# Token mixers among the projection tiles of a decoder trunk, and half of the last normalisation on GpSimd

## The reference

```
h = x @ w_in                    # 2816 columns: ret q,k,v,gate | swa q,k,v | conv value,gate | sgu u,v
A  retention, 4 heads x 64: chunks of 128 rows, a = (q k^T) * decay, o = a v + (q S) * q_dec,
   S = S * c_dec + (k * k_dec)^T v ; group norm of o, times silu(gate)
B  attention, 4 heads x 64, causal, log-multiplicity bias; the samples also read cached keys and values
C  val * sigmoid(gate) -> depthwise convolution of width 31 -> layer norm over 256 channels -> silu
D  u, v = gelu ; group norm of v ; u * (W_s v + b) within 128 rows
x = layer_norm(alpha * x + concat(A, B, C, D) @ w_out)
x = layer_norm(alpha * x + moe(x))          # best 1 of 4 groups, then best 2 of its 8 experts
```

## Time and profile before

| | |
|---|---|
| median of 3 runs (lowest to highest) | 1935.23 us (1932.53 to 1937.45) |
| the profiled execution's own time | 1938.98 us |
| its span in the profile | 1936.9 us |
| its mean granted clock of TensorE | 0.854 |
| busy: PE, weight load, DVE, ACT, POOL | 76%, 52%, 28%, 11%, 21% |
| moved by DMA | 532.60 MB, mean 275 GB/s |

### The profile page before, as it was taken

One profiled execution on the slowest core, in us unless ns is written; L12 is line 12 of the kernel. 1 busy time (PEld: TensorE's weight loads), 2 busy tenths in 40 slices (PEclk: granted clock), 3 DMA queues, 4 the chain that ended last, 5 costly groups with the idle time before them and its releaser, 6 DMA issues. The chain is left out here.

```text
span 1936.9 us, 40042 instructions
## 1 busy us (share of the span) xinstructions
PE 1472.9 (76%) x16276; PEld 1012.2 (52%) x16276; DVE 544.6 (28%) x1215; ACT 208.8 (11%) x579; POOL 398.8 (21%) x533
## 2 busy tenths in 40 slices
PE   8998899949567576767499988995766758566990
PEld 7887647835334333434488874684433424333550
DVE  0395352541000000000609735236100101000116
ACT  2111030001000000000121112201000000000010
POOL 3149230111001011100311943001211101110113
PEclk9999589969788888879699977896878878887995
DMA  8711041949999999999531102265899999999824
GB/s 341 280 66 58 1 159 64 364 173 359 428 425 382 425 426 425 384 425 386 194 135 66 44 36 109 92 256 225 333 427 425 380 427 424 426 425 425 349 89 142
DMA packets 77409, 532.60 MB, mean 275 GB/s; under 512 B 14430, under 2 KB 31770, under 8 KB 48538
## 3 DMA queue, kind: packets, MB, share of 16 engines
q1 hardware_dynamic: 45466, 482.00, 60.4%
q0 software_dynamic: 11136, 35.40, 5.0%
q10 hardware_dynamic: 20736, 14.18, 2.3%
HBM read 772.37 MB, written 35.98 MB: 417 GB/s over the span
## 5 line engine op out<-in xcount | busy, mean ns | idle before, releaser
L871 PE MATMUL ps<-arena,xT 128*32 128x256 f32 x6912 | 477.8, 437 | 252.1 <-DMA arena<-in_w 250.5
L871 PEld LDWEIGHTS ps<-arena,xT 128*32 128x32 f32 x6912 | 274.9, 126 | 444.7 <-issue 352.9
L542 PE MATMUL ps<-arena,xT 128*128 128x256 f32 x1920 | 424.9, 382 | 0.9 <-issue 0.9
L542 PEld LDWEIGHTS ps<-arena,xT 128*128 128x128 f32 x1920 | 363.9, 191 | 51.5 <-issue 1.0
L1496 DVE COPY xT<-ps 128x128 f32<-128x128 f32 x108 | 31.5, 291 | 907.2 <-PE ps L880 907.2
L889 PE MATMUL ps<-arena,xT 128*32 128x256 f32 x3456 | 212.2, 386 | 34.0 <-DVE xT L1496 22.4
L1674 POOL COPY xT<-xT 128x1 int32 x108 | 19.7, 182 | 805.8 <-PE ps L861 805.8
L889 PEld LDWEIGHTS ps<-arena,xT 128*32 128x32 f32 x3456 | 108.7, 110 | 110.2 <-issue 27.2
L1676 POOL DMA_INDIRECT xT<-x1d,xT x108 | 105.0, 972 | 53.1 <-POOL xT L1674 49.6
L1106 DVE SCALAR_TENSOR_TENSOR arena<-arena 128x784 f32<-128x784 f32 x120 | 113.7, 1029 | 0.0
L1017 ACT ACTIVATE xT<-ps 128x128 f32<-128x128 f32 x108 | 30.0, 278 | 668.7 <-PE ps L871 668.7
(11 more groups left out here) (244 smaller groups left out, 1223.1 us busy)
## 6 DMA issues: line engine op xcount, KB each, us to landing
arena<-in_w SPq DMA_DIRECT2D x324, 2048.0 KB
arena<-in_w_proj SPq DMA_DIRECT2D x30, 1024.0 KB, 5.0
arena<-in_kv SPq DMA_DIRECT2D x32, 640.0 KB, 5.1
yd<-xT ACTq DMA_DIRECT2D x432, 32.0 KB
yd<-arena POOLq DMA_DIRECT2D x22, 512.0 KB, 18.6
rowpar<-in_rowpar SPq DMA_DIRECT2D x2, 2708.0 KB, 17.2
x1d<-arena SPq DMA_DIRECT2D x8, 512.0 KB, 14.6
arena<-x1d SPq DMA_DIRECT2D x8, 512.0 KB, 6.7
```

The lines of the kernel that those rows point to most:

```text
L542: ins = pe.matmul(bank[0:n, 0:CW], xT[:, k, 128 * t:128 * t + n], ring[slot(c)][:, k, :], start=(k == 0), stop=(k == KT - 1))
L871: ins = pe.matmul(HB[q][r, 0:256], xgT[q][:, k % 2, BLK * (k // 2):BLK * (k // 2 + 1)], w13[q][:, :, k, 128 * j:128 * (j + 1)], start=(k = ...
```

## The change

**Chunks and tiles.** The chunks are taken in another order (VAL, GATE, SQ, SK, SV, RQ, RK, V, RV, U, RG). `chunk` becomes `tile(c, t)`, one row tile of one chunk, on two PSUM banks instead of five (`ps[2]`, `ps[3]`), which leaves `ps[4]` to `ps[7]` to the mixers while projections still run. The ring has one slot that is used once (chunk 2) and two that alternate. PE's list is now: VAL, GATE pairs; SQ, SK, SV with the GLU and attention transposes between; the attention loop with one tile of RQ, RK or V in each unit, the convolution's transposes in units 10 to 14, and the samples' keys, probabilities and values in units 1, 3, 8, 9, 12 and 14; then retention with tiles of RV and U; gating; RG's tiles between the turned rows; the output projection.

**Places.** The transposed heads get buffers of their own in the arena, where x and the fourth cache slot lie (`sT`, `rT`). So x is overwritten and loaded again before the output projection: layer 0 from `x_in`, layer 1 from a DRAM copy `x2d` that SP stores tile by tile in the passage.

**Engines.** The SWA rotation, key decay and retention's norm go from POOL to DVE, the query copies from POOL to ACT; DVE's taps are cut into pieces, 38 before attention and the rest in units 0 to 8. POOL's rotation is six operations for all tiles instead of four for each tile and two. V is copied out and its GELU done at once, behind attention.

**Routing.** 50 products without use (`run_idle`) stand in PE's list in front of three waits.

**The passage.** DVE does the first half only, POOL the second, in two operations.

```diff
+TAPS_AT = (38, 41, 44, 47, 50, 53, 54, 57, 59, 62)
...
@@ SP @@
+                if L:
+                    for t in range(TILES):
+                        sp.wait_ge(sem("x2"), (L - 1) * TILES + t + 1)
+                        sp.dma_start(x2d[128 * t:128 * t + ROWS[t], :], x[0:ROWS[t], t, :]).then_inc(sem("x_saved"), 16)
...
+                ring_load(7)
+                for i in range(2 * NKV, 3 * NKV):
+                    kv_load(i)
+                ring_load(8)
+                for i in range(3 * NKV, 4 * NKV):
+                    kv_load(i)
+                ring_load(9)
+                ring_load(10)
                 E.need("ret_upd", 4)
...
+                E.need("smp_o", 1)
+                E.need("qb_ok", 1)
+                for t in range(TILES):
+                    rows = slice(128 * t, 128 * t + ROWS[t])
+                    sp.dma_start(x[0:ROWS[t], t, :], x2d[rows, :] if L else io["x_in"][rows, :]).then_inc(sem(f"x_in{t}"), 16)
                 E.need("smp_upd", 1)
...
+                E.need("sgu_vn", 1)
...
+                for c in range(NCH, NCH + NOUT):
                     ring_load(c)
@@ PE @@
+                def tile(c, t):
+                    if t == 0:
                         pe.wait_ge(sem(f"ring{slot(c)}"), filled(c, L))
+                    j = serial(c, t, True)
+                    if j >= 2:
+                        E.need("proj_out", j - 1)
+                    E.done(weigh(ps[2 + j % 2], c, t), "proj")
...
+                E.need("s_act", 4)
+                E.need("proj_out", (SV + 1) * TILES)
+                att_scores(0)
+                for u in range(16):
+                    if u < 15:
+                        att_scores(u + 1)
+                    if u > 10:
+                        E.need("conv_out", u - 10)
+                    if u:
+                        tile(RQ + (u - 1) // TILES, (u - 1) % TILES)
+                    if 10 <= u < 15:
+                        turn_conv(u - 10, RQ * TILES + u - 1)
+                    att_turn(u)
+                    if u:
+                        att_values(u - 1)
+                    if u == 1:
+                        new_key_scores()
+                        cached_key_scores(range(0, NKV))
+                    if u == 3:
+                        cached_key_scores(range(NKV, NB))
+                    if u == 8:
+                        turn_sample_probs()
+                    if u == 9:
+                        sample_values(range(0, NKV))
+                    if u == 12:
+                        sample_values(range(NKV, NB))
+                    if u == 14:
+                        sample_back()
...
+                for n in range(4):
+                    E.need("ret_a", n + 1)
+                    if n < 3:
+                        ret_scores(n + 1)
+                    if n:
+                        E.need("ret_upd", n)
+                    ret_products(n)
+                    ret_rows(n)
+                    tile((RV, RV, U, U)[n], (3, 4, 0, 1)[n])
...
+                for t in range(2, TILES):
+                    turn_mix(t - 2)
+                    tile(RG, t)
+                turn_mix(3)
...
+                def run_idle(n):
+                    for k in range(n):
+                        pe.matmul(HIDDEN[:, 0:256], ident, ones2, start=True, stop=True)
+
+                run_idle(18)
                 E.need("member", 1)
...
+                run_idle(28)
                 E.need("onehot", 1)
...
+                run_idle(4)
                 E.need("which", 1)
@@ DVE, the attention loop and behind it @@
+                for u in range(16):
+                    if u:
+                        total_inverse(u - 1)
+                    if u < 15:
+                        attend(u + 1)
+                    if u < 9:
+                        taps(TAPS_AT[u], TAPS_AT[u + 1])
...
+                    if u == 15:
...
+                        centre(conv, TILES, 256, rstat)
+                    if u:
+                        att_rows(u - 1)
...
+                mask_scores(0)
+                spread(conv, TILES, 256, rstat)
+                E.need("v_act", 1)
+                centre(sv, ng, HD, pstat)
+                for n in range(4):
+                    if n < 3:
+                        mask_scores(n + 1)
...
+                    E.done(ins, "ret_upd")
+                    E.need("ret_upd", n + 1)
+                    if n == 0:
+                        scaled(conv, TILES, 256, rstat, 1)
+                    if n == 1:
+                        spread(sv, ng, HD, pstat)
+                    if n == 2:
+                        E.link(along(conv, RP("conv_ln_g"), ALU.mult))
+                        E.done(along(conv, RP("conv_ln_b"), ALU.add), "conv_norm")
...
+                centre(rows, 16, HD, rows_stat)
+                spread(rows, 16, HD, rows_stat)
+                scaled(sv, ng, HD, pstat, 2)
+                E.need("smp_o", 1)
...
+                E.link(along(sv, RP("sgu_ln_g"), ALU.mult))
+                E.done(along(sv, RP("sgu_ln_b"), ALU.add), "sgu_vn")
@@ the passage: DVE, then POOL @@
+                def centred_gain(t):
+                    n = ROWS[t]
+                    xs = x[0:n, t, :]
+                    E.done(dve.scalar_tensor_tensor(out=xs, in0=xs, scalar=mv[0:n, t, 0:1], in1=RP("ln2_g")[0:n, :],
+                                                    op0=ALU.subtract, op1=ALU.mult), "x2_gain")
...
                     if t:
-                        row_norm(t - 1, "ln2_g", "ln2_b", "x2_pow", "x2")
-                row_norm(TILES - 1, "ln2_g", "ln2_b", "x2_pow", "x2")
+                        centred_gain(t - 1)
+                centred_gain(TILES - 1)
...
+                def rows_done(t):
+                    n = ROWS[t]
+                    E.need("x2_pow", t + 1)
+                    E.need("x2_gain", t + 1)
+                    xs = x[0:n, t, :]
+                    E.link(pool.tensor_tensor(xs, xs, mv[0:n, t, 2:3].to_broadcast([n, D]), ALU.mult))
+                    E.done(pool.tensor_tensor(xs, xs, RP("ln2_b")[0:n, :], ALU.add), "x2")
+
                 for t in range(TILES):
...
                     E.done(pool.tensor_tensor(mv[0:n, t, 2:3], mv[0:n, t, 3:4], halfc[0:n, 0:1], ALU.pow), "x2_pow")
+                    if t:
+                        rows_done(t - 1)
+                rows_done(TILES - 1)
```

More of the change, by code:

```diff
@@ L420, in _ @@
                 E.done(sp.dma_start(out, ret_state), "stores", 16)
-                for c in range(NCH + 2, NCH + NOUT):
+                E.need("sgu_vn", 1)
+                out = io["s_sgu"][bass.ds(L, 1)].rearrange("a p c -> (a p) c")
+                E.done(sp.dma_start(out, h[0:NS, V, 4, :]), "stores", 16)
+                for c in range(NCH, NCH + NOUT):
                     ring_load(c)
@@ L564, in _ @@
+                tile(SQ, 0)
+                tile(SQ, 1)
                 E.need("glu", 1)
@@ new lines, in _, with ret_scores @@
+                E.need("smp_rows", 1)
+                E.need("smp_y", 1)
+                turn_pair(RQ, RK, "r_tr", lambda k: (("r_act", "r_dve")[k % 2], k // 2 + 1))
+                tile(RV, 1)
+                def ret_scores(n):
+                    for hd in range(NH):
+                        hp, hh = hd // 2, hd % 2
+                        ins = pe.matmul(ps[4 + hh][:, hp * 128:(hp + 1) * 128], rT[half(hh), 2 + hp, n * 128:(n + 1) * 128],
+                                        rT[half(hh), hp, n * 128:(n + 1) * 128], start=True, stop=True)
+                    E.done(ins, "ret_s")
@@ new lines, in _ @@
+                E.done(ins, "smp_o1")
+                tile(U, 2)
+                E.need("ret_a", 5)
+                E.need("smp_o1c", 1)
+                for hd in range(NH):
+                    pe.matmul(ps[0][0:NS, hd * HD:(hd + 1) * HD], sm[0][0:NS, hd * NS:(hd + 1) * NS],
+                              h[0:NS, RV, 4, hd * HD:(hd + 1) * HD], start=True, stop=False)
+                    ins = pe.matmul(ps[0][0:NS, hd * HD:(hd + 1) * HD], sm[1][0:64, hd * NS:(hd + 1) * NS],
+                                    ident[0:64, 0:64], start=False, stop=True)
@@ new lines, in _ @@
+                E.need("vexp", 1)
+                for hd in range(NH):
+                    hp, hh = hd // 2, hd % 2
+                    ins = pe.matmul(ps[4 + hp][half(hh), :], h[0:NS, RK, 4, hd * HD:(hd + 1) * HD],
+                                    vexp[:, hd, :, :].rearrange("p b e -> p (b e)"), start=True, stop=True)
+                E.done(ins, "smp_o")
+                tile(U, 3)
+                tile(U, 4)
+                E.need("sgu_vn", 1)
+                E.need("sgu_w", 1)
+                wT = CP("sgu_wT").rearrange("p (g t) -> p g t", g=4)
@@ L975, in _ @@
-                E.need("qk_tr", 9)
-                E.done(act.copy(xT[:, 0:8, SEQ:NTOK], ps[0][:, 0:8 * NS].rearrange("p (k n) -> p k n", k=8)), "qk_act")
+                for t in range(TILES):
+                    turn_out(t, (0, 1))
+                    if t:
```

(20 more changed lines are left out.)

923 lines of the change are left out of this document (449 added, 474 removed).

## The result

| | before | changed |
|---|---|---|
| median | 1936.34 us (4 runs) | 1879.61 us (1878.47 to 1882.45, 4 runs) |
| ratio, 95% interval | | 0.9712 (0.9693 to 0.9731) |
| the profiled execution's own time, span | 1938.98, 1936.9 us | 1880.68, 1878.8 us |

The change makes the kernel 2.9% faster. The forecast was 1885 (1858 to 1914), for a faster kernel: 50 us were to go, and 57 went by the medians, 58 in the profiles. The sum came out well, but not all of its terms did, as the stages show. Each is measured between the same two events of both profiles, and the column of differences adds up to the 58.1 us of the spans.

A forecast was written before the change was run, and what follows sets the result against it. Mixers were held back by TensorE's clock and gaps, experts by weight transfers. Terms -30 - 33 - 5 + 7 + 11 = -50 took the profiled 1938.98 us to 1889, or 1885 against the median; range 1858 to 1914.

The forecast's parts named there:

- The mixers: Projections through turned rows in each layer: interleaved tiles save clock and gaps, -30 us in layer 0, -33 in layer 1.
- work that is left: Layer 0's mixer stretch if TensorE never waits and keeps 2.4 GHz: 219.0 us against 267.2, so at most 48 won.
- Layer 1's bound of 50: Layer 1's mixer stretch: at most 50 us to be won, from which 16 us of new waits were taken.
- The new waits: Mixers: waits of TensorE that the new order makes, 18.5 us in layer 0 and 16 in layer 1.
- the second pass of transposes: Mixers: two passes of head transposes instead of one, one emptied by ScalarE alone, the other behind a GELU: 5 us.
- POOL's rotations: Attention: POOL's twelve retention rotations meet VectorE's convolution taps of units 6 to 8: 3 us.
- Routing: Idle products before three waits speed up the index product and first expert block: -2.5 us a layer (+2 to -4).
- The passage: Last normalisation: POOL and VectorE take turns, not overlap: +7 us between the layers, +11 at the end.
- POOL's halves hide: Rival 1, last normalisation: POOL's work overlaps VectorE's, as the power rows suggest; 1868 us; chance 0.13.
- VectorE becomes the bound: Rival 2, mixers: VectorE's longer list and POOL's powers lose 12 to 15 us a layer; 1912 us; chance 0.15.
- The clock stays down: Rival 3, interleaved stretch: it stays at 1.2 GHz as long as now, losing 31 us a layer; 1947 us; chance 0.07.
- All loads late: Rival 4: a cache or ring wait in each layer, a few us, within the range; no chance of its own.

The follow-up runs named there:

- e5: The kernel before with seven idle products in the gap ahead of its head transposes, in each layer: 1929.88 us, ratio 0.9991.
- e6: The kernel before with e5's seven idle products and eight more ahead of each retention chunk's rows: 1948.32 us, ratio 1.0074.
- e12: The changed kernel with the old order of the eight cached samples, taken two at a time as in the kernel before: 1892.53 us, ratio 0.9789.
- e10: The changed kernel with the last normalisation on VectorE again and idle products filling TensorE's gaps, no useful work moved: 1850.05 us, ratio 0.9580.
- e7: The changed kernel itself, run again beside e8 and others on one chip: 1878.57 us, ratio 0.9719 to the kernel before.
- e1: The changed kernel with both halves of the last normalisation on VectorE again, in the passage and at the end: 1861.19 us, ratio 0.9627.
- e8: The same edit as e1, repeated beside the changed kernel on one chip: 1859.92 us, ratio 0.9622.
- e2: The changed kernel without the 50 idle products in routing: 1881.66 us, ratio 0.9730.

## Why the prediction was right, and where it was not

- **The mixers, -30 and -33; measured -33.2 and -40.1.** The mechanism holds: the clock came back because dense tiles stand among narrow products (0.95 and 0.97 against 0.88; e5 and e6 show that it was the narrow products, not the gap). The first step failed: "the number of tiles does not change, only their places", and with it the 219.0 us of "work that is left". At full clock the work is about 208.5: in layer 0 219.46 busy us at 0.95, in layer 1 214.56 at 0.97. The cached samples' products, 10.5 us a layer of it, had been halved by their order, and e12 shows that some 12 of the 73 us (trace), or 14 (times), are theirs. Without them the two layers gave about -29 and -32, what was forecast. (Layer 1's bound of 50 has no rows behind it; worked out like layer 0's, 267.4 - 248.38 x 0.88, it is 48.8.)
- **The new waits, 18.5 and 16; they were idle for 13.7 and 12.0 us.** Named right: GLU 2.5 (2.81), first softmax 4 (4.06), `sgu_vn` and `ret_upd` 4 (2.29). Too large: the second pass of transposes, 5 (about 2.3), and POOL's rotations, 3 (one wait of 1.3 on VectorE; of POOL's twelve operations of 640 columns three took 2.1 to 2.3 beside the taps, the others 1.5). Missing from the list: the price of the clock behind each gap, 0.05 x 219 = 11 us in layer 0 and 6 in layer 1. The bound had been worked out at full clock and only waits were set against it. That the term still came out near is in part luck: in layer 0 10.5 us of work that had gone and 4.8 of waits that were too dear stand against 11 of clock that were left out (29.5 + 10.5 + 4.8 - 11 = 33.8, measured 33.2).
- **Routing, -2.5 a layer; measured -0.3 and -0.4.** The index product came as forecast. Of the 5.0 us that were to be paid back (4.6 by the rows, since 6.04 less 3.66 is 2.4 and not 2.7), the product gave 2.2, and 1.5 went back because the 28 products overran VectorE. The first block was read as going to 3.66; it went to 5.35. A shorter one would not have helped: from its start to VectorE's first sum it is 508.8 us in e10, where the block takes 3.66, and 509.3 here. And TensorE comes to routing 0.8 later in this profile, its fourth turn at half clock behind 2.1 us of idling. That is not the change's doing: in e7, the same list, this way is 19.4 us and not 21.3, and in e5, with the old routing, 19.4 too. So the size of this term is not resolved, only that it is small.
- **The passage, +7 and +11; measured +5.4 and +10.8.** Taking turns was the right rule, and the power operations, which spoke for 1 us, the wrong row. The period came out at 7.3 us a tile, not 8.4, since the statistics don't take turns; at the end that hardly counts, for there POOL runs alone. The rule of the Trainium skill (SBUF — State Buffer, section Who interferes with whom) agrees here with its own restriction too: it is the two-input operations of VectorE that are held (4.11 against 2.60), not the statistics (1.29).
- **Rivals.** POOL's halves hide: e1 and e8 refute it. VectorE becomes the bound: no wait on it was over 2.3 us. The clock stays down: it did in e5, where nothing dense stood in between; here it was 0.80 at its worst in 15 us. All loads late: one cache wait of 0.97 us. Of the signs that were named, the tail, the index product and POOL's bias came; the clock from 100 to 270 us was 0.95 and not near 1.0, and the first expert block was not near 3.7.

What stays open: where in a stretch the clock falls differs from one execution to the next. From 200 to 215 us it was 0.80 in the changed kernel's profile and 1.00 in e7, with the same list. The traces show that it does, not why. And no run takes the moves between engines (rotation, key decay and retention's norm from POOL to VectorE) apart from the interleaving: what they gave or cost alone is not shown.

## What to carry to other kernels

Look for time in TensorE's busy periods too: multiply them by the granted clock, and where narrow products stand together at half of it, put dense work that has to be done anyway between them. Idle products are for gaps alone, above all ahead of narrow products on the critical path, and never longer than the gap. An idle GpSimd is no free help for VectorE where VectorE's operations read two tensors in SBUF, least of all at the end, where nothing hides its longer operations; and when a change reorders small products, count them again, for which strips are neighbours can halve their time.

## What the runs showed that I had not expected

- 32 products of 128x32 weights took 2.36 us with neighbours in four strips, and 16 took 2.35 with neighbours in two.
- Retention's 64-column products brought the clock to 0.50 for 30 us although TensorE was busy for 29 of them (e5), straight behind ten us at 0.99.
- The same instructions behind the same kind of gap cost differently from one execution to the next. In e2 a gap of 3.16 us was followed by transposes at 1.09, in the changed kernel one of 2.81 by transposes at 1.97. The whole stretch of layer 0 varied by 5.7 us between executions of the same list.
